# Down projection of a decoder block: PSUM banks copied by ScalarE and added by accumulating DMAs, and a seven-product scheme on 4 of 8 row blocks

## The chip, the cores and the metric

The kernel runs on one core of a Trainium2 chip. The metric is the device time of one execution in microseconds (us).

## The reference, cut to what matters

One layer of a hybrid decoder on 256 tokens of width 2048, in float32: three token mixers, merged by gates, and then a squared-ReLU MLP. The change touches the MLP's second half alone, the down projection from 8192 to 2048.

```python
h = rmsnorm(x, norm_ffn_g[l])
x = x + jnp.square(jax.nn.relu(h @ w_up[l])) @ w_down[l]     # w_up 2048x8192, w_down 8192x2048
return rmsnorm(x, final_g)
```

## The kernel before

Every matmul multiplies float32 numbers that are split into a high part (rounded to the float32r type) and a low part (the remainder); a product of two such numbers is three matmuls: high by high, high by low, low by high. TensorE (PE) does only these.

**Slabs.** All weights stream from HBM in slabs of 512 KB through a ring of four places in `w_raw`. For each slab, in order: SyncE issues the load (`load_slab`), ScalarE (ACT) copies the raw slab to `w_hi` (`hi`, L504), VectorE (DVE) writes `w_lo` as raw minus high (`lo`, L736), and PE multiplies (12 matmuls in the down projection). At PE's slab k, ACT and DVE prepare slab k+3 (`LOOKAHEAD`). The load of slab s is issued once `lo` of slab s-4 is done. Every engine walks the same loops (`walk`) in the order in which the code is written; each works through its own list, and semaphores join them.

**The MLP** runs in 4 chunks of 2048 hidden columns. A chunk has 4 trips of the up projection (`up`, 8 slabs each, two groups of 4: `n` = 0 and 1) and 2 trips of the down projection (`down`, 16 slabs each; a trip is called a pair here, since it makes two blocks of 512 output columns, `n` = 0 and 1, in turn, in the order of `PAIR` and `PAIR_ENDS`). When an up group ends, ACT copies half of its sums (`second`, L667), and DVE runs a chain over it: add (L1207), scale (L1209, which frees the PSUM banks: `evac_done`), squared ReLU (L1258), for n = 1 also the sums of activations that the seven-product scheme takes (`a_sums`, L808 to L813, and their low part, L818), and the low part of the hidden values (L1264).

**The seven-product scheme.** Two slabs of the same rows, of column blocks 0 and 1, hold four 128x512 blocks; with the two token blocks that is a 2x2 by 2x2 block product. It takes 8 products, 24 matmuls; `products_quad` takes 7, 21 matmuls, after a scheme of the Strassen-Winograd kind. It needs sums of weights: DVE makes four (`forms_first`, L747; `forms_second`, L754 and L757) into `w_sums`, ACT copies them to their high part (`forms_hi`, L510 and L512), and DVE takes the low part (`forms_lo`, L763, in two parts). A place where two slabs are done so is called a quad and named by its first slab in the trip; `quads` lists them. Of a quad's products three go into the corner banks (4 to 7) and four into banks of their own (P1, P6, P7, P5 in banks 0 to 3), which are added into several blocks of the output at the end of the trip.

**The sums at the end of a pair** are DVE's: `corner_sums` adds banks 4 to 7 to the token rows `y_tok` (L797, twice), `token_sums` adds P1, P5, P6 and P7 (L779 to L790, six instructions) after ACT has copied P1 (`first_product`, L519).

PE waits for `lo_done` at each slab, for `t_lo` (the forms' low part) at the second and the sixth product of a quad, and for `evac_done` at the first slab of each column block.

Of the kernel before, what the change touches and what calls it, by code (L numbers as in the profile page):

```python
# [27 lines left out]
P = 128  # L28
# [81 lines left out]
PAIR = [(0, 0), (0, 1), (1, 0), (1, 1), (0, 2), (1, 2), (0, 3), (1, 3), (0, 4), (1, 4), (0, 5), (1, 5)]  # L110
# [4 lines left out]
P_SUMS = 5  # L115
# [14 lines left out]
def quads(ph, c, t):  # L130

    if ph.name != "down":
        return ()
    return (6,) if last_trip(ph, c, t) else (6, 10, 14)


def quad_of(ph, c, t, k):

    return c * (3 * PH["down"].trips) + t * 3 + quads(ph, c, t).index(k)
# [23 lines left out]
def walk(eng, body):  # L163

    def loop(name, c=0, first=0):
        with eng.Fori(first, PH[name].trips) as t:
# [12 lines left out]
    for t in range(PH["A"].trips):  # L179
        body(PH["A"], 0, t)  # L180
    for t in range(PH["mix"].trips):
        body(PH["mix"], 0, t)
    def chunk(c):
        body(PH["up"], c, 0)
        loop("up", c, first=1)
        for t in range(PH["down"].trips):
            body(PH["down"], c, t)

    chunk(0)
    with eng.Fori(1, CHUNKS - 1) as c:  # L190
        chunk(c)
    chunk(CHUNKS - 1)
# [16 lines left out]
def build(nc, x, norm_mix_g, w_in, gate_b, conf_dw, conf_ln_g, conf_ln_b, w_conf_out, sconv_w,  # L209
# [5 lines left out]
    with ctx:  # L215
# [62 lines left out]
        v_now = sb("v_now", [P, 2, HD])  # L278
        mask = sb("mask", [P, SC])
# [51 lines left out]
        c_full, p_one, p_sum, p_last = sem("c_full"), sem("p_one"), sem("p_sum"), sem("p_last")  # L331
        gf_in, y_sq, y_gain = sem("gf_in"), sem("y_sq"), sem("y_gain")
# [153 lines left out]


        @block.scalar
        def _(act):
# [24 lines left out]
            def first_product(ph, c, t, k):  # L514

                if not (isinstance(c, int) and c == 0 and isinstance(t, int) and t == 0):
                    act.wait_ge(p_sum, P_SUMS * pair_of(c, t))
# [111 lines left out]
            def trip(ph, c, t):  # L629
                if ph == "v tokens":  # L630
                    return
                for k in range(ph.nslabs):
                    hi(ph, c, t, k)
                    forms_hi(ph, c, t, k)
                    if ph.name == "down" and k == quads(ph, c, t)[-1] + 1:
# [73 lines left out]
                    if last_trip(ph, c, t):  # L709
                        if k in (3, 4):  # L710
                            act.wait_ge(p_sum, P_SUMS * pair_of(c, t))
                            for b in range(2):
                                y_squared(b, k - 3, 2 * (k - 3) + b)
# [10 lines left out]
        def _(dve):  # L724
# [40 lines left out]

            def token_sums(c, t):

                base = P_SUMS * pair_of(c, t)
                g = group_of(PH["down"], c, t, 0)
                last = last_trip(PH["down"], c, t)  # L770
                cols = [bass.ds(t * 2 * DCOLS + n * DCOLS, DCOLS) for n in range(2)]
                rows2 = y_tok[:, 1, bass.ds(t * 2 * DCOLS, 2 * DCOLS)].rearrange("p (n w) -> p n w", n=2)
                p6, p7, p5 = (acc[:, P_BANK[name], :] for name in ("P6", "P7", "P5"))
                read, count = (p_last, 1) if last else (half_sum, 2)
                dve.wait_ge(p_one, pair_of(c, t) + 1)
                dve.wait_ge(slab_used, slab_of(PH["down"], c, t, quads(PH["down"], c, t)[-1] + 1) + 1)
# [14 lines left out]

            def corner_sums(c, t):

                for n in range(2):
                    cols = bass.ds(t * 2 * DCOLS + n * DCOLS, DCOLS)
                    dve.wait_ge(c_full, pair_of(c, t) * 2 + n + 1)
                    dve.tensor_tensor(y_tok[:, :, cols], acc[:, 4 + 2 * n:6 + 2 * n, :], y_tok[:, :, cols],  # L797
                                      ALU.add).then_inc(evac_done, 1)
# [214 lines left out]
            def final_block(c, t):  # L1013
# [33 lines left out]
                dve.wait_ge(p_sum, P_SUMS * (pair_of(c, t) + 1))  # L1047
# [16 lines left out]
                scale(1, 0)  # L1064

            def trip(ph, c, t):
# [4 lines left out]
                for k in range(ph.nslabs):  # L1071
# [22 lines left out]
                    if ph.name == "up" and k == 0 and isinstance(t, int) and not (isinstance(c, int) and c == 0):  # L1094
                        token_sums(c - 1, PH["down"].trips - 1)
                    if k + 4 in quads(ph, c, t):
                        forms_first(ph, c, t, k + 4)
# [8 lines left out]
                    if last_trip(ph, c, t):  # L1106
                        if k == 8:
                            token_sums(c, t)
                        if k in (9, 10):
                            dve.wait_ge(p_sum, P_SUMS * pair_of(c, t))  # L1110
# [168 lines left out]
        def _(pe):  # L1279
# [75 lines left out]
            def products_quad(ph, c, t, k):  # L1355
# [34 lines left out]
                if first and not (isinstance(c, int) and c == 0 and isinstance(t, int) and t == 0):  # L1390
                    pe.wait_ge(p_sum, pair_of(c, t) * P_SUMS)
# [217 lines left out]
```

## Time and profile before

| | us |
|---|---|
| median of 3 runs | 1515.77 (1515.49 to 1516.7) |
| the profiled execution | 1514.95 |
| its span | 1513.2 |
| PE busy | 1502.0 |
| DVE busy | 1188.9 |
| ACT busy | 755.7 |
| GpSimd (POOL) busy | 2.0 |

The span runs from the first to the last instruction of the profiled execution; its own time is 1.75 us longer. Busy times of PE are of overlapping, pipelined matmuls.

### The profile page before, as it was taken

To read this page: it belongs to the slowest core of one execution; us is meant where nothing else is said; L and a number is where in the kernel's file an instruction comes from. 1 tells how busy PE (TensorE), PEld (TensorE's weight loads), DVE (VectorE), ACT (ScalarE), POOL (GpSimd) and SP (SyncE) were. 2 spreads that over 40 slices of the span, in tenths; PEclk is the share of its full clock that TensorE was granted. 3 is DMA by queue.
4 is the path that set the end of the run, shared out by engine and by line. 5 is a ranking of instruction groups with operands and counts; after the bars stand their busy time and mean duration, and the time that the engine had idled before them with its cause. 6 is when DMAs were issued, how large, how long until landed. Compare 5 with 4: busy or idle time off the path is not lost.

```text
span 1513.2 us, 22156 instructions
## 1 busy us (share of the span) xinstructions
PE 1502.0 (99%) x7645; PEld 1267.4 (84%) x7645; DVE 1188.9 (79%) x1573; ACT 755.7 (50%) x940; POOL 2.0 (0%) x11
## 2 busy tenths in 40 slices
PE   9999999999999999999999999999999999999997
PEld 7888888877778888888888888888888888888886
DVE  6668889988889877565656779987799778987797
ACT  6444444465554455444445445544554545544554
POOL 0000000000000000000000000000000000000000
PEclk9999999999999999999999999999999999999999
DMA  7655666655555666665555565655556555556563
GB/s 251 190 187 185 192 194 195 199 177 173 171 173 192 192 197 208 195 200 191 189 185 167 184 205 203 201 182 193 190 199 207 182 192 196 208 181 208 195 219 144
DMA packets 209967, 290.94 MB, mean 192 GB/s; under 512 B 9227, under 2 KB 129107, under 8 KB 209778
## 3 DMA queue, kind: packets, MB, share of 16 engines
q1 hardware_dynamic: 209906, 290.14, 58.6%
q8 instruction: 37, 0.61, 0.2%
q14 instruction: 24, 0.20, 0.0%
HBM read 287.48 MB, written 2.10 MB: 191 GB/s over the span
## 4 chain that ended last, share of the span: by engine, by line
PE 99%; DVE 0%; ACT 0%; DMA 0%; issue 0%; DVEq 0%; ACTq 0%
PE acc L1309 27%; PE acc L1328 16%; PE acc L1330 15%; PE acc L1329 15%; PE acc L1307 13%; PE acc L1376 2%; PE acc L1377 2%; PE acc L1375 2%; PE acc L1302 2%; PE acc L1399 1%; PE acc L1304 1%; PE acc L1453 0%; PE acc L1475 0%; PE acc L1349 0%; PE acc L1348 0%; PE acc L1347 0%
## 5 line engine op out<-in xcount | busy, mean ns | idle before, releaser
L504 ACT ACTIVATE w_hi<-w_raw 128x1024 fp32r<-128x1024 f32 x511 | 534.0, 1057 | 477.4 <-PE acc L1330 285.3
L736 DVE TENSOR_TENSOR w_lo<-w_raw,w_hi 128x1024 fp32r<-128x1024 f32 x511 | 616.7, 1222 | 180.4 <-ACT w_hi L504 176.2
L1309 PE MATMUL acc<-h_hl,w_hi 128*128 128x512 f32 x1740 | 546.7, 395 | 0.0
L1307 PEld LDWEIGHTS acc<-h_hl,w_lo 128*128 128x128 f32 x1740 | 322.3, 188 | 72.4 <-issue 0.6
L1307 PE MATMUL acc<-h_hl,w_lo 128*128 128x256 f32 x1740 | 343.6, 279 | 0.0
L1309 PEld LDWEIGHTS acc<-h_hl,w_hi 128*128 128x128 f32 x1740 | 265.2, 189 | 0.0
L1328 PE MATMUL acc<-w_hi,m_hl 128*128 128x512 f32 x448 | 174.6, 390 | 0.0
L1330 PE MATMUL acc<-w_hi,m_hl 128*128 128x512 f32 x448 | 174.3, 389 | 0.0
L1329 PE MATMUL acc<-w_lo,m_hl 128*128 128x512 f32 x448 | 174.3, 389 | 0.0
L1328 PE MATMUL acc<-w_hi,h_hl 128*128 128x512 f32 x384 | 151.5, 394 | 0.0
L1330 PE MATMUL acc<-w_hi,h_hl 128*128 128x512 f32 x384 | 149.6, 389 | 0.0
L1329 PE MATMUL acc<-w_lo,h_hl 128*128 128x512 f32 x384 | 149.5, 389 | 0.0
L876 DVE SCALAR_TENSOR_TENSOR conv<-glu,par,conv (+1 forms) x240 | 109.1, 481 | 7.0 <-DVE conv L876 5.8
L1329 PEld LDWEIGHTS acc<-w_lo,m_hl 128*128 128x128 f32 x448 | 84.1, 188 | 17.4
L1330 PEld LDWEIGHTS acc<-w_hi,m_hl 128*128 128x128 f32 x448 | 84.1, 188 | 17.4
L1328 PEld LDWEIGHTS acc<-w_hi,m_hl 128*128 128x128 f32 x448 | 84.1, 188 | 17.4
L1328 PEld LDWEIGHTS acc<-w_hi,h_hl 128*128 128x128 f32 x384 | 72.1, 188 | 17.1 <-DVE w_lo L736 2.7
L667 ACT ACTIVATE second<-acc 128x512 f32<-128x512 f32 x58 | 34.7, 599 | 101.9 <-PE acc L1309 101.9
L1330 PEld LDWEIGHTS acc<-w_hi,h_hl 128*128 128x128 f32 x384 | 72.1, 188 | 15.2
L1329 PEld LDWEIGHTS acc<-w_lo,h_hl 128*128 128x128 f32 x384 | 72.1, 188 | 14.6
L1207 DVE TENSOR_TENSOR pair<-acc,second 128x512 f32<-128x512 f32 x54 | 37.3, 691 | 55.3 <-ACT second L667 55.3
L704 ACT ACTIVATE m_hl<-pair 128x512 f32 (+1 forms) x32 | 20.2, 632 | 73.6 <-DVE pair L1258 73.6
(208 smaller groups left out, 1472.9 us busy)
## 6 DMA issues: line engine op xcount, KB each, us to landing
w_raw<-in_w_in SPq DMA_DIRECT2D x200, 512.0 KB, 3.6
w_raw<-in_w_up SPq DMA_DIRECT2D x128, 512.0 KB, 4.3
w_raw<-in_w_down SPq DMA_DIRECT2D x128, 512.0 KB, 4.1
w_raw<-in_w_mix_out SPq DMA_DIRECT2D x32, 512.0 KB, 3.5
w_raw<-in_w_sconv_out SPq DMA_DIRECT2D x16, 512.0 KB, 4.2
w_raw<-in_w_attn_out SPq DMA_DIRECT2D x16, 512.0 KB, 3.6
w_raw<-in_w_conf_out SPq DMA_DIRECT2D x16, 512.0 KB, 4.6
bias_row<-in_gate_b SPq DMA_DIRECT2D x12, 256.0 KB, 4.0
```

The costliest lines, as they stand in the source:

```text
L504: act.activation(w_hi[:, q], w_raw[:, q], ACT.Copy).then_inc(hi_done, 1)
L667: act.activation(second[:, :, :], acc[:, b:b + 2, SEQ:], ACT.Copy).then_inc(half_copied, 1)
L736: dve.tensor_tensor(w_lo[:, q], w_raw[:, q], w_hi[:, q].bitcast(F32), ALU.subtract).then_inc(lo_done, 1)
L876: dve.scalar_tensor_tensor(dst, src, w, dst, ALU.mult, ALU.add).then_inc(step, 1)
L1207: dve.tensor_tensor(dst, halves[0], second[:, :, :], ALU.add).then_inc(half_sum, 1)
L1302: pe.matmul(*wide[m], start=True, stop=False)
L1307: pe.matmul(*narrow[m], start=False, stop=False)
L1309: last = pe.matmul(*wide[m], start=False, stop=final)
L1328: pe.matmul(acc[:, b + m, :], h_h, hi[:, a, :], start=first, stop=False)
L1329: pe.matmul(acc[:, b + m, :], h_h, lo[:, a, :], start=False, stop=False)
L1330: last = pe.matmul(acc[:, b + m, :], h_l, hi[:, a, :], start=False, stop=final)
L1375: pe.matmul(acc[:, at, :], rows[0], columns[0], start=start, stop=False)
```

## The change

The last two of an up chunk's slabs and the last two of a down trip now carry the forms of the next trip's first quad (`next_block`), so that each pair but the very last has quads at slabs 2, 6, 10 and 14 in place of 6, 10 and 14: that is 4 of 8 row blocks. `PAIR` changes the order of the first four slabs for that: column block 1 is begun at slab 1 in place of slab 2. The last up trip of a chunk is taken out of the loop. The very last pair keeps its one quad and its sums on DVE.

For the other seven pairs, `corner_sums` and `token_sums` are replaced. ACT copies banks 4 to 7 at slab 15 (`corner_copies`, two instructions) and P1 and P5 at slab 0 of what follows (`p_copies`, two). DVE makes P1+P6 and P1+P6+P7 (`partial_sums`, two). GpSimd issues eight accumulating DMAs a pair, from SBUF to SBUF: two of 512 KB, then three of 256 KB once these two have landed, then three of 256 KB once those have. ACT's next corner copies wait until all eight have landed, and so do the closing sums of the last pair.

The diff, cut to its core:

```diff
-PAIR = [(0, 0), (0, 1), (1, 0), (1, 1), (0, 2), (1, 2), (0, 3), (1, 3), (0, 4), (1, 4), (0, 5), (1, 5)]
+PAIR = [(0, 0), (1, 0), (0, 1), (1, 1), (0, 2), (1, 2), (0, 3), (1, 3), (0, 4), (1, 4), (0, 5), (1, 5)]
...
-    return (6,) if last_trip(ph, c, t) else (6, 10, 14)
+    return (6,) if last_trip(ph, c, t) else (2, 6, 10, 14)
...
         body(PH["up"], c, 0)
-        loop("up", c, first=1)
+        loop("up", c, first=1, last=1)
+        body(PH["up"], c, PH["up"].trips - 1)
...
+            def add_to(dst, src):
+                pool.dma_start(dst, src, accum_op=ALU.add).then_inc(y_acc, 16)
+
+            def trip(ph, c, t):
+                before = 16 * ADDS * pair_of(c, t)
+                cols = [slice((2 * t + n) * DCOLS, (2 * t + n + 1) * DCOLS) for n in range(2)]
+                for n in range(2):
+                    pool.wait_ge(evac_done, group_of(ph, c, t, n) + 1)
+                    add_to(y_tok[:, :, cols[n]], corner[n][:, :, :])
+                pool.wait_ge(p_copied, 2 * pair_of(c, t) + 2)
+                pool.wait_ge(y_acc, before + 32)
+                add_to(y_tok[:, 0, cols[0]], p1_copy[:, :])
+                for b in range(2):
+                    add_to(y_tok[:, b, cols[1]], p5_copy[:, :])
+                pool.wait_ge(p_sum, pair_of(c, t) + 1)
+                pool.wait_ge(y_acc, before + 80)
+                add_to(y_tok[:, 0, cols[1]], p16[:, :])
+                for n in range(2):
+                    add_to(y_tok[:, 1, cols[n]], p167[:, :])
...
+            def corner_copies(c, t):
+
+                if not (isinstance(c, int) and c == 0 and t == 0):
+                    act.wait_ge(y_acc, 16 * ADDS * pair_of(c, t))
+                for n in range(2):
+                    act.wait_ge(c_full, pair_of(c, t) * 2 + n + 1)
+                    act.activation(corner[n][:, :, :], acc[:, 4 + 2 * n:6 + 2 * n, :], ACT.Copy).then_inc(evac_done, 1)
+
+            def p_copies(c, t):
+
+                act.wait_ge(slab_used, slab_of(PH["down"], c, t, 15) + 1)
+                act.activation(p1_copy[:, :], acc[:, P_BANK["P1"], :], ACT.Copy).then_inc(p_copied, 1)
+                act.activation(p5_copy[:, :], acc[:, P_BANK["P5"], :], ACT.Copy).then_inc(p_copied, 1)
...
+            def partial_sums(c, t):
+
+                g = group_of(PH["down"], c, t, 0)
+                dve.wait_ge(p_copied, 2 * pair_of(c, t) + 2)
+                dve.tensor_tensor(p16[:, :], acc[:, P_BANK["P6"], :], p1_copy[:, :], ALU.add).then_inc(half_sum, 2)
+                dve.wait_ge(half_sum, g + 2)
+                dve.tensor_tensor(p167[:, :], acc[:, P_BANK["P7"], :], p16[:, :], ALU.add).then_inc(p_sum, 1)
...
+            def next_block(ph, t, k):
+
+                if ph.name == "up" and isinstance(t, int) and t == ph.trips - 1 and k >= ph.nslabs - 2:
+                    return PH["down"], 0, k - ph.nslabs
+                if ph.name == "down" and t < ph.trips - 1 and k >= ph.nslabs - 2:
+                    return ph, t + 1, k - ph.nslabs
+                return ph, t, k
...
-                    if k + 3 in quads(ph, c, t):
-                        forms_second(ph, c, t, k + 3)
-                    if ph.name == "down" and k == 15 and not last_trip(ph, c, t):
-                        corner_sums(c, t)
+                    down, to, at = next_block(ph, t, k)
+                    if at + 3 in quads(down, c, to):
+                        forms_second(down, c, to, at + 3)
                     lo(ph, c, t, k)
                     if ph.name == "down" and k == 0 and t:
-                        token_sums(c, t - 1)
+                        partial_sums(c, t - 1)
...
-                    if k + 4 in quads(ph, c, t):
-                        forms_first(ph, c, t, k + 4)
+                    if at + 4 in quads(down, c, to):
+                        forms_first(down, c, to, at + 4)
                     if k + 2 in quads(ph, c, t):
                         forms_lo(ph, c, t, k + 2, 0)
```

What this does to DVE's list is shown where a chunk passes from up to down (chunk 0). Before, the last up trip is in a loop (its end is the branch of L166), and the down trip begins with three `lo` and the forms of quad 6:

```order
600 L818 ISA [waits f_hi]
601 L818 TENSOR_TENSOR a_forms<-pair,a_forms 128x512
602 L166 REGISTER_ALU
603 L166 COMPARE_AND_BRANCH
604 L736 TENSOR_TENSOR w_lo<-w_raw,w_hi 128x1024 [waits hi_done] x3
605 L747 TENSOR_TENSOR w_sums<-w_raw 128x1024 [waits raw_full3,raw_full2]
606 L754 TENSOR_TENSOR w_sums<-w_raw,w_sums 128x512 [waits t_raw]
607 L757 TENSOR_TENSOR w_sums<-w_raw,w_sums 128x512 [waits t_two]
608 L736 TENSOR_TENSOR w_lo<-w_raw,w_hi 128x1024 [waits hi_done]
609 L733 TENSOR_TENSOR w_lo<-w_raw,w_hi 128x512 [waits hi_done]
610 L763 TENSOR_TENSOR w_forms<-w_sums,w_forms 128x1024 [waits t_hi]
```

In the changed kernel the end of the last up trip reads on DVE as follows (L786 is `lo`, L797 to L807 the forms' sums, L1257 the first step of the chain after an up group):

```order
609 L786 TENSOR_TENSOR w_lo<-w_raw,w_hi 128x1024 [waits hi_done] x3
610 L797 TENSOR_TENSOR w_sums<-w_raw 128x1024 [waits raw_full3,raw_full2]
611 L804 TENSOR_TENSOR w_sums<-w_raw,w_sums 128x512 [waits t_raw]
612 L807 TENSOR_TENSOR w_sums<-w_raw,w_sums 128x512 [waits t_two]
613 L786 TENSOR_TENSOR w_lo<-w_raw,w_hi 128x1024 [waits hi_done]
614 L1257 TENSOR_TENSOR pair<-acc,second 128x512 [waits half_copied,slab_used]
615 L1259 TENSOR_TENSOR pair<-pair,rstd 128x512 [waits half_sum]
616 L1308 SCALAR_TENSOR_TENSOR pair<-pair 128x512 [waits evac_done]
```

Three instructions on `w_sums` now stand between the sixth and the last `lo` of the up trip. Behind the chain follow, still on DVE, its last two steps, the first `lo` of the down trip (half a slab, L783) and the low part of the forms (L813):

```order
621 L1314 TENSOR_TENSOR m_hl<-pair,m_hl 128x2x256 [waits hid_hi]
622 L862 TENSOR_TENSOR a_forms<-pair,a_forms 128x512 [waits f_hi]
623 L783 TENSOR_TENSOR w_lo<-w_raw,w_hi 128x512 [waits hi_done]
624 L813 TENSOR_TENSOR w_forms<-w_sums,w_forms 128x1024 [waits t_hi]
625 L786 TENSOR_TENSOR w_lo<-w_raw,w_hi 128x1024 [waits hi_done]
626 L813 TENSOR_TENSOR w_forms<-w_sums,w_forms 128x1024 [waits t_hi]
627 L786 TENSOR_TENSOR w_lo<-w_raw,w_hi 128x1024 [waits hi_done]
```

On PE, the changed kernel's list from the third slab of that first down trip on (L1425 to L1427 are a quad's matmuls; `w_forms` in a row is a form of the weights):

```order
2510 L1380 MATMUL acc<-w_hi,m_hl 128x512
2511 L1425 MATMUL acc<-w_hi,m_hl 128x512 [waits lo_done,hid_lo]
2512 L1426 MATMUL acc<-w_lo,m_hl 128x512
2513 L1427 MATMUL acc<-w_hi,m_hl 128x512
2514 L1425 MATMUL acc<-w_forms,m_hl 128x512 [waits t_lo]
2515 L1426 MATMUL acc<-w_forms,m_hl 128x512
```

The wait for `t_lo` stands before the 28th matmul of the trip now; before, the first one stood before the 76th.

## Rows read from the trace of the kernel before

**Rows 1.** The page: the span, and PE's busy time, share and instructions.

```profile
span 1513.2 us, 22156 instructions
PE 1502.0 (99%) x7645; PEld 1267.4 (84%) x7645; DVE 1188.9 (79%) x1573; ACT 755.7 (50%) x940; POOL 2.0 (0%) x11
```

**Rows 2.** Waits of PE: the latest of its three (total, times, longest us).

```profile
PE acc L1302 <- DVE w_lo L829: 0.4, 1, 0.4
```

**Rows 3.** Timeline of PE: first matmuls of chunk 0's down and quad (start, us).

```profile
904.10 0.39 PE L1328 MATMUL acc<-w_hi,m_hl 128*128 128x512 f32 x1
...
920.43 0.39 PE L1375 MATMUL acc<-w_hi,m_hl 128*128 128x512 f32 x1
```

**Rows 4.** Line L1377: matmuls with a form of weights and plain activations.

```profile
L1377 PE MATMUL acc<-w_forms,m_hl x22: 389/389/389, 921.6 to 1479.9; 128*128 128x512 f32 x22
```

**Rows 5.** Timeline of DVE from the end of chunk 0's up on.

```profile
905.01 0.69 DVE L1207 TENSOR_TENSOR pair<-acc,second 128x512 f32<-128x512 f32 x1 [1.18 <-ACT second L667]
905.74 0.69 DVE L1209 TENSOR_TENSOR pair<-pair,rstd 128x512 f32<-128x512 f32 x1
...
909.96 3.50 DVE L736 TENSOR_TENSOR w_lo<-w_raw,w_hi 128x1024 fp32r<-128x1024 f32 x3
914.79 1.23 DVE L747 TENSOR_TENSOR w_sums<-w_raw 128x1024 f32<-128x1024 f32 x1 [1.34 <-DMA w_raw<-in_w_down]
...
917.39 1.22 DVE L736 TENSOR_TENSOR w_lo<-w_raw,w_hi 128x1024 fp32r<-128x1024 f32 x1
918.52 0.68 DVE L733 TENSOR_TENSOR w_lo<-w_raw,w_hi 128x512 fp32r<-128x512 f32 x1
919.13 1.22 DVE L763 TENSOR_TENSOR w_forms<-w_sums,w_forms 128x1024 fp32r<-128x1024 f32 x1
```

**Rows 6.** Timeline of ACT over the same stretch.

```profile
908.88 2.94 ACT L504 ACTIVATE w_hi<-w_raw 128x1024 fp32r<-128x1024 f32 x3
...
917.50 1.07 ACT L510 ACTIVATE w_forms<-w_sums 128x1024 fp32r<-128x1024 f32 x1 [1.62 <-DVE w_sums L757]
```

**Rows 7.** The load issued at 899.01, its landing, and that of the load at 901.28.

```profile
899.01 0.37 SPq L413 DMA_DIRECT2D w_raw<-in_w_down  x1
DMA to landing us min/median/max: 3.5/3.5/3.5
DMA to landing us min/median/max: 5.5/5.6/5.7
```

**Rows 8.** Timeline of DVE between chunk 0's two pairs.

```profile
942.19 1.22 DVE L736 TENSOR_TENSOR w_lo<-w_raw,w_hi 128x1024 fp32r<-128x1024 f32 x1 [0.36 <-ACT w_hi L504]
943.33 2.35 DVE L797 TENSOR_TENSOR y_tok<-acc,y_tok 128x1024 f32<-128x1024 f32 x2
...
948.09 0.68 DVE L779 TENSOR_TENSOR y_tok<-p_part,y_tok 128x512 f32<-128x512 f32 x1
...
953.14 2.36 DVE L736 TENSOR_TENSOR w_lo<-w_raw,w_hi 128x1024 fp32r<-128x1024 f32 x2
```

**Rows 9.** Timeline of ACT and of PE in the same place.

```profile
944.78 0.58 ACT L519 ACTIVATE p_part<-acc 128x512 f32<-128x512 f32 x1
945.85 1.06 ACT L504 ACTIVATE w_hi<-w_raw 128x1024 fp32r<-128x1024 f32 x1 [0.50 <-PE acc L1377]
945.59 0.39 PE L1328 MATMUL acc<-w_hi,m_hl 128*128 128x512 f32 x1
```

**Rows 10.** Busy times over the second pair (PE, PEld, DVE, ACT, POOL; clock, DMA share, GB/s).

```profile
945.80:986.90 41.10, 41.10 (x183) 34.02 (x182) 38.40 (x39) 22.08 (x23) 0.00 (x0) 1.00 0.61 199
```

**Rows 11.** DMA issues: the copies from SBUF to SBUF, KB each, us to landing.

```profile
k_dup<-pair SPq DMA_DIRECT2D x4, 128.0 KB, 2.4
```

**Rows 12.** Timeline of DVE: last sums of the last but one pair, first of the last.

```profile
1460.45 2.35 DVE L797 TENSOR_TENSOR y_tok<-acc,y_tok 128x1024 f32<-128x1024 f32 x2
...
1486.03 0.68 DVE L779 TENSOR_TENSOR y_tok<-p_part,y_tok 128x512 f32<-128x512 f32 x1
```

**Rows 13.** PE's last matmul, and the us in which its granted clock fell.

```profile
1505.08 0.39 PE L1349 MATMUL acc<-w_hi,m_hl 128*128 128x512 f32 x1
1508.00:1509.00 1.00, 0.00 (x0) 0.00 (x0) 0.75 (x1) 0.95 (x1) 0.00 (x0) 0.70 0.03 8
```

More of the change, by code:

```diff
@@ L114 @@
 S1, S2, S3, S4 = range(4)
-P_SUMS = 5
+ADDS = 8
 def last_trip(ph, c, t):
@@ L133, in quads @@
         return ()
-    return (6,) if last_trip(ph, c, t) else (6, 10, 14)
+    return (6,) if last_trip(ph, c, t) else (2, 6, 10, 14)
 def quad_of(ph, c, t, k):
-    return c * (3 * PH["down"].trips) + t * 3 + quads(ph, c, t).index(k)
+    return c * (4 * PH["down"].trips) + t * 4 + quads(ph, c, t).index(k)
 def pair_of(c, t):
@@ L163, in walk, with loop @@
 def walk(eng, body):
-    def loop(name, c=0, first=0):
-        with eng.Fori(first, PH[name].trips) as t:
+    def loop(name, c=0, first=0, last=0):
+        with eng.Fori(first, PH[name].trips - last) as t:
             body(PH[name], c, t)
@@ L278, in build @@
         v_now = sb("v_now", [P, 2, HD])
+        copies_at = nc.lookup_mloc(probs).addr
+        assert [nc.lookup_mloc(b).addr - copies_at for b in (probs_t, q_now, k_now)] == [4 * 1536, 4 * 2304, 4 * 2816]
+        corner = [view(f"corner{n}", probs, 2 * n * DCOLS, [P, 2, DCOLS]) for n in range(2)]
+        p1_copy, p5_copy = (view(f"p{i}_copy", probs, (4 + n) * DCOLS, [P, DCOLS]) for n, i in enumerate((1, 5)))
+        p16, p167 = (view(f"p_{i}", k_dup, n * DCOLS, [P, DCOLS]) for n, i in enumerate(("two", "three")))
         mask = sb("mask", [P, SC])
@@ L485, in _ @@
                                fill=MASKED, base=-1, pattern=[[1, BLK]], channel_multiplier=-1).then_inc(consts, 1)
+            def add_to(dst, src):
[16 more added lines that the diff above has]
+                    add_to(y_tok[:, 1, cols[n]], p167[:, :])
+            for c in range(CHUNKS):
+                for t in range(PH["down"].trips):
+                    if not last_trip(PH["down"], c, t):
+                        trip(PH["down"], c, t)
         @block.scalar
@@ L632, in trip @@
                 for k in range(ph.nslabs):
+                    if ph.name == "down" and k == 15 and not last_trip(ph, c, t):
+                        corner_copies(c, t)
                     hi(ph, c, t, k)
+                    if ph.name == "down" and k == 0 and t:
+                        p_copies(c, t - 1)
+                    if ph.name == "up" and k == 0 and isinstance(t, int) and t == 0 and not (isinstance(c, int) and c == 0):
+                        p_copies(c - 1, PH["down"].trips - 1)
                     forms_hi(ph, c, t, k)
-                    if ph.name == "down" and k == quads(ph, c, t)[-1] + 1:
+                    if last_trip(ph, c, t) and k == quads(ph, c, t)[-1] + 1:
                         first_product(ph, c, t, k)
@@ L1390, in products_quad @@
                 if first and not (isinstance(c, int) and c == 0 and isinstance(t, int) and t == 0):
-                    pe.wait_ge(p_sum, pair_of(c, t) * P_SUMS)
+                    pe.wait_ge(p_sum, pair_of(c, t))
+                    pe.wait_ge(p_copied, 2 * pair_of(c, t))
                 product(P_BANK["P1"], whole(0, 2 * i), loaded(w_x, 0), first, final).then_inc(slab_used, 1)
```

42 lines of the change are left out of this document (14 added, 28 removed).

## The prediction

> **What bounds the kernel now.** The page comes first: PE is busy for 1502.0 of 1513.2 us [rows 1]. Its waits come next, since a busy share alone doesn't say that nothing is lost: the latest wait of PE is at the first slab of all [rows 2], so from about 11 us to its last matmul at 1505 us PE never stops. Time is then the number of matmuls times their spacing. The spacing is read from the timeline, not from the 0.39 us of one, as they overlap: from 904.10 to 920.43 there are six slabs of 12, so 16.33 / 72 = 0.227 us [rows 3]. All other engines matter only where they would make PE wait, and for that the question is always the same: when is a thing ready, and when does PE ask for it?
>
> **What it takes away.** A quad saves 3 matmuls of 24. The line of the quads' third matmuls counts 22 quads, by the one form-by-plain product in each [rows 4]: 7 pairs of 3 and one of 1. With 4 in each of 7 pairs it is 29. So 7 x 3 x 0.227 = 4.76 us less, 0.31% of the time. That is all that can be won; the sums that leave DVE (2.3 us at 943.33 and 5.05 us from 948.09 to 953.14 in each pair [rows 8]) are work beside PE and worth nothing by themselves. A measurement of this kernel can tell about 0.2%, 3 us, from no change.
>
> **The new first quad, up to down.** This is the place on which I stake the number. Call 904.10 the start of the down trip in chunk 0 [rows 3]. PE asks for the forms at its 28th matmul, 904.10 + 27 x 0.227 = 910.22. When are they ready? DVE goes through its list in order:
> - the forms' first sum needs the slab that was issued at 899.01 and landed 3.5 us later [rows 7], so it starts at about 902.6;
> - from such a sum to the `lo` behind the second sums it is 917.39 - 914.79 = 2.60 us, and that `lo` takes 1.13 to the next instruction [rows 5]: the chain after the up group, which began at 905.01, begins at 906.33, that is 1.32 us late;
> - the chain lasts 909.96 - 905.01 = 4.95 us [rows 5]: 911.28;
> - half a `lo` 0.61 (918.52 to 919.13), the forms' low part 1.22 [rows 5]: 913.11.
>
> ACT is no earlier: its first copy behind the chain began at 908.88, with the shift 910.20; half a copy of about 0.6 and the forms' copy of 1.07 [rows 6] give 911.87, just when DVE wants it. So PE stands for 913.11 - 910.22 = 2.89 us. Part of it is paid earlier: column block 1 is now begun at slab 1, at 904.10 + 12 x 0.227 = 906.82, and its banks are freed when L1209 ends, at 906.43 before and 907.75 with the shift [rows 5], so 0.93 us at slab 1 and the other 1.96 at the quad. It isn't added, since DVE's chain doesn't wait for these slabs. After it, the second part of the forms (one `lo` of 1.13 and 1.22 more: 915.4) is asked for 12 matmuls after 913.11, at 915.8, so it holds by 0.4 us. The other chunks have the same list: 4 x 2.89 = 11.6 us.
>
> Bounds of this term: with the slab there in time the chain isn't shifted at all, and 905.01 + 4.95 + 0.61 + 1.22 = 911.79 still leaves 1.57 us, 6.3 in all. With the landing of 5.6 us that a load behind two others took [rows 7] it is 2.1 us more, 5.0 each and 20 in all. I take 3.5 us, as this very load had it alone in flight.
>
> **The new first quad, down to down** (4 times). DVE's `lo` at 942.19 ends its step at 943.33 [rows 8]. Then: the sums of the forms 2.60, a `lo` 1.13, half a one 0.61, `partial_sums` two adds of 0.72, the low part 1.22: 950.3. PE asks at 945.59 + 27 x 0.227 = 951.7 [rows 9], so 1.4 us are left. ACT has two corner copies of 1.06 where it had nothing, and two bank copies of 0.58 where it had one [rows 9]; from c_full at about 942.4 its list is copy, copy, high part (to 945.6), half a high part at 945.85 [rows 9], two bank copies, forms (to 948.7), each before DVE needs it. The next quad needs DVE for about 9.1 of PE's 10.2 us. Cost: nothing; if the cover is gone, each us of DVE's lateness beyond 1.4 is a us of PE, four times. PE's wait for the P banks (`p_copied`, `p_sum`, done by 949.1) is 9 matmuls into the quad, at 953.1, and costs nothing.
>
> **The accumulating DMAs.** The trace has none. A pair adds 2 x 512 + 6 x 256 KB, 2.62 MB. Over a pair the loads keep the DMA engines 61% busy at 199 GB/s [rows 10], so 326 GB/s when busy, and 2.62 MB are 8.0 us of all 16 engines if an add costs as a load does. The spare time in a pair is 0.39 x 41.1 = 16.0 us. So they fit, even where an add costs twice; from there on they don't. A copy from SBUF to SBUF took 2.4 us to land [rows 11]; three rounds of that with 8 us of transfer are some 15 to 20 us. ACT asks for them a pair later (41 us), and in the last pair DVE asks at 1486.03, 25.6 us after the corner sums of the pair before [rows 12]. I take nothing for it; the other end, twice the cost and loads pushed back, is a rival below.
>
> The Trainium skill ("Collectives: The Full Stack", The bandwidth ceiling) says that an add in the DMA engines needs two source reads where a copy needs one and so runs at half the rate. By it a pair's adds would be 16 us of all engines, and the spare time would be just used up; no row here shows an add. The Trainium skill ("SBUF — State Buffer", SBUF: two separate sides) also says that VectorE's two-port modes lock GpSimd out while it writes descriptors; the instructions of DVE in the down trips are adds of two tensors, 1.22 us for 1024 columns, which show no such mode, so by it nothing would be late.
>
> **The sum.** 1514.95 - 4.76 + 11.6 = 1521.8 for an execution like the profiled one, which lay 0.8 us below the median; against the median 1522.6. The last up trip is out of its loop, which spares a few tenths of register work in its chain. Predicted: 1522 us, 0.4% slower.
>
> **Rivals.**
> - *Slower still, by the DMA engines* (12 in 100). Where an add costs twice, pairs with adds beside quads are full, the loads' landing goes from 3.5 towards 5.6 us and more, and DVE, which already waited for a slab at 914.79, gets late: against it, the spare 1.4 us and the reading above; for it, bursts of loads landed at 5.6 us even before. If four pairs lose a tenth of their 41 us, 16 us: 1538. A few us in the last pair alone (DVE waits for the adds) would be 1526.
> - *Slower still, by the clock* (8 in 100). PE has no stop in the trace after the start; at the end its granted clock fell in the us after 1508, some 2.9 us after its last matmul had ended [rows 13]. A stop of 2.9 us in two parts, with work between them, is hardly that. If it fell, the 18 matmuls left of the quad would go at 1.2 in place of 2.4 GHz, 4.1 us a chunk: 1538.
> - *No change* (12 in 100). The stop is near its lower bound of 1.57 us, since the slab is early: 4 x 1.57 - 4.76 is +1.5 us, 1517.
> - *Faster* (13 in 100). The forms are ready in time: 1511. It would need DVE's way from 905.01 to the low part to be 5.2 us where the rows add to 6.8 without any shift; it is decided at 1.19 us of stop in each chunk, the point at which stops and saving are equal. For it speaks only that DVE and ACT lose other work there, and the token sums before were far from this place.
> - *My forecast* (55 in 100): 1517.5 to 1526, most at 1522.
>
> Slower by over 0.2% (above 1518.8) hold the forecast and the first two rivals: 0.75. Within 0.2%: 0.12. Faster: 0.13. The range leaves out the fast case and the worst of the slow ones: 1514 to 1530.
>
> **What would show it.** Waits of PE in the changed trace: for DVE's `w_forms` (L813) four times at about 2 us, and at the second slab of each chunk's first down trip for about 0.9 us; DVE's chain L1257 beginning 1.3 us later after the slab before the down trip; first sums (L797) idle for a DMA there. No wait of PE between the two pairs of a chunk. 29 quads at L1427. Loads landing at about 4 us. The prediction is wrong if PE shows no waits there, or if the longest waits are for slabs (`lo`) in the pairs.

## The result, and the profile after

The changed kernel took 1530.93 us (median of 4 runs, 1530.8 to 1534.11) against 1515.99 us (4 runs, 1515.49 to 1516.7) on the same chip: a ratio of 1.0104, 95% interval 1.0092 to 1.0116. It is slower by 15 us where 7 were predicted, and 0.9 us beyond the range. The profiled execution took 1530.8 us.

The page of the changed kernel, its span, PE's busy time, two DMA queues (packets, MB, share of 16 engines) and the landing of the largest adds (KB each, median us from issue to landing):

```profile
span 1529.0 us, 22058 instructions
PE 1503.1 (98%) x7624; PEld 1263.3 (83%) x7624; DVE 1177.2 (77%) x1566; ACT 781.0 (51%) x975; POOL 55.6 (4%) x67
...
q1 hardware_dynamic: 209906, 290.14, 59.7%
q0 software_dynamic: 9856, 18.35, 6.9%
...
y_tok<-corner POOLq DMA_DIRECT2D x14, 512.0 KB, 8.8
```

PE has its 21 matmuls less than in [rows 1] (7645 to 7624) and is not less busy. The last matmul, at 1505.08 before [rows 13], now starts at 1521.18 (the last row of PE's timeline below). It is 16.10 us later although 21 x 0.227 = 4.77 us of work are gone: PE stands 20.9 us more than before. I call this sum the *stops* of a kernel (the shift of its last matmul against 1505.08, plus 0.227 us for each matmul fewer than 7645; up to 0.6 us of it is the start, which differs from run to run). It is the quantity that every experiment below takes apart. The waits of PE name the first places (us in all, times, longest):

```profile
PE acc L1378 <- DVE pair L1259: 5.4, 4, 2.0
PE acc L1425 <- DVE w_forms L813: 5.2, 5, 1.5
PE acc L1397 <- DVE w_lo L786: 3.5, 3, 2.1
```

Where [rows 2] ended at the first slab, there are now waits for VectorE in three kinds of place. They don't add to 20.9, since this view leaves small waits out, so I also went along PE's timeline and took every start that came over 0.227 us behind the one before: 13.4 us at the first quads of the four chunks (the large ones are 2.15 and some 1.75 in chunk 0, the latter spread over matmuls at the lower clock, and 1.41 + 1.62, 1.29 + 1.64, 1.23 + 1.57 in the others), 2.1 us in the second pairs of chunks 0 to 2, where the large ones stand at the quad of slab 6 and none at that of slab 2, and 4.4 us at the closing products of the last pair.

**The timelines.** That of DVE at chunk 0's way from up to down, at its second pair, and ahead of the last token sums (start, us, the idle time before in brackets):

```profile
897.97 3.50 DVE L786 TENSOR_TENSOR w_lo<-w_raw,w_hi 128x1024 fp32r<-128x1024 f32 x3 [0.26 <-ACT w_hi L536]
904.04 1.23 DVE L797 TENSOR_TENSOR w_sums<-w_raw 128x1024 f32<-128x1024 f32 x1 [2.57 <-DMA w_raw<-in_w_down]
...
907.77 0.68 DVE L1257 TENSOR_TENSOR pair<-acc,second 128x512 f32<-128x512 f32 x1
...
913.13 1.23 DVE L813 TENSOR_TENSOR w_forms<-w_sums,w_forms 128x1024 fp32r<-128x1024 f32 x1 [0.17 <-ACT w_forms L542]
...
960.69 1.23 DVE L797 TENSOR_TENSOR w_sums<-w_raw 128x1024 f32<-128x1024 f32 x1 [3.41 <-DMA w_raw<-in_w_down]
...
1496.58 1.22 DVE L786 TENSOR_TENSOR w_lo<-w_raw,w_hi 128x1024 fp32r<-128x1024 f32 x1 [0.62 <-ACT w_hi L536]
1502.09 0.69 DVE L833 TENSOR_TENSOR y_tok<-p_part,y_tok 128x512 f32<-128x512 f32 x1 [4.29 <-DMA y_tok<-p_three]
```

and of PE, in chunk 0 and at the end:

```profile
906.95 0.39 PE L1380 MATMUL acc<-w_hi,m_hl 128*128 128x512 f32 x1
909.33 0.47 PE L1378 MATMUL acc<-w_hi,m_hl 128*128 128x512 f32 x1 [1.99 <-DVE pair L1259]
...
911.31 0.63 PE L1379 MATMUL acc<-w_lo,m_hl 128*128 128x512 f32 x1
...
914.43 0.48 PE L1425 MATMUL acc<-w_forms,m_hl 128*128 128x512 f32 x1
...
1508.42 0.50 PE L1397 MATMUL acc<-w_hi,m_hl 128*128 128x512 f32 x1 [2.15 <-DVE w_lo L786]
...
1521.18 0.39 PE L1399 MATMUL acc<-w_hi,m_hl 128*128 128x512 f32 x1
```

From up to down the mechanism is the predicted one: the slab for the first sum is waited for, the chain after the up group starts late (907.77 instead of 905.01 [rows 5]), and PE stands at the second slab for its banks.

In the second pair DVE waits 3.41 us for a load at the first sum of the quad at slab 6. In the last pair it waits for an add, and PE then for the slab's low part behind it. Where that add was, the chain that ended last shows (start, us, what):

```profile
1470.89 1.95 ACT corner L557 x2
1472.84 0.71 POOL y_tok L495
1473.55 10.68 DMA y_tok<-corner
1484.27 0.51 issue
1484.78 1.12 POOL y_tok L495 x2
1485.90 5.77 DMA y_tok<-p_copy
1491.71 0.49 issue
1492.20 1.08 POOL y_tok L495 x2
1493.28 8.79 DMA y_tok<-p_three
1502.09 0.69 DVE y_tok L833
```

The three rounds of adds take 28.5 us, from 1473.55, when the second add of the first round starts, to 1502.07. DVE asked for them at 1496.58 + 1.22 = 1497.80. Two of DVE's waits in all (us, times, longest):

```profile
DVE w_sums L797 <- DMA w_raw<-in_w_down: 30.7, 19, 3.4
DVE y_tok L833 <- DMA y_tok<-p_three: 4.3, 1, 4.3
```

The first of them is the other trace of the adds. The first sums of the quads waited 10.5 us in 15 places before (L747); now it is 30.7 us in 19. The load behind the wait of 3.41 us was issued at 951.43, while two adds of 512 KB were under way (issued at 947.40 and 948.31, landed at 953.38 and 958.27). From issue to landing it took, in the changed kernel and in e1 below, which has no adds and issues it at 951.55:

```profile
DMA to landing us min/median/max: 9.1/9.1/9.1
DMA to landing us min/median/max: 4.9/4.9/4.9
```

### The profile page after: what moved, and what is told of

The parts are those of the page before. It is cut to its first block, busy times and chain, and to the rows that moved or that the text cites. A ratio compares the mean times of both kernels' runs of the same rounds, so it can differ in the third digit from the quotient of the medians.

```text
span 1529.0 us, 22058 instructions
## 1 busy us (share of the span) xinstructions
PE 1503.1 (98%) x7624; PEld 1263.3 (83%) x7624; DVE 1177.2 (77%) x1566; ACT 781.0 (51%) x975; POOL 55.6 (4%) x67
## 3 DMA queue, kind: packets, MB, share of 16 engines
q0 software_dynamic: 9856, 18.35, 6.9%
## 4 chain that ended last, share of the span: by engine, by line
PE 82%; DMA 8%; DVE 7%; issue 2%; ACT 1%; SPq 0%; POOL 0%; DVEq 0%; ACTq 0%; POOLq 0%
PE acc L1359 25%; PE acc L1357 12%; PE acc L1378 12%; PE acc L1380 12%; PE acc L1379 12%; DMA w_raw<-in_w_down 6%; DVE w_lo L786 2%; PE acc L1352 2%; PE acc L1425 2%; PE acc L1426 1%; PE acc L1427 1%; DVE w_sums L797 1%; PE acc L1450 1%; PE acc L1354 1%; DVE w_sums L804 1%
## 5 line engine op out<-in xcount | busy, mean ns | idle before, releaser
L536 ACT ACTIVATE w_hi<-w_raw 128x1024 fp32r<-128x1024 f32 x504 | 527.1, 1056 | 462.0 <-PE acc L1380 258.2
L786 DVE TENSOR_TENSOR w_lo<-w_raw,w_hi 128x1024 fp32r<-128x1024 f32 x504 | 609.9, 1222 | 197.8 <-ACT w_hi L536 189.6
L1378 PE MATMUL acc<-w_hi,m_hl 128*128 128x512 f32 x392 | 153.8, 392 | 5.4 <-DVE pair L1259 5.4
L1380 PE MATMUL acc<-w_hi,m_hl 128*128 128x512 f32 x392 | 153.2, 391 | 0.0
L1379 PE MATMUL acc<-w_lo,m_hl 128*128 128x512 f32 x392 | 153.0, 390 | 0.0
L1378 PEld LDWEIGHTS acc<-w_hi,m_hl 128*128 128x128 f32 x392 | 73.7, 188 | 22.1 <-issue 3.8
L1380 PEld LDWEIGHTS acc<-w_hi,m_hl 128*128 128x128 f32 x392 | 73.9, 189 | 15.5
L1379 PEld LDWEIGHTS acc<-w_lo,m_hl 128*128 128x128 f32 x392 | 73.9, 188 | 15.2
L1378 PEld LDWEIGHTS acc<-w_hi,h_hl 128*128 128x128 f32 x384 | 72.1, 188 | 17.1 <-DVE w_lo L786 2.7
L1380 PEld LDWEIGHTS acc<-w_hi,h_hl 128*128 128x128 f32 x384 | 72.1, 188 | 15.2
L813 DVE TENSOR_TENSOR w_forms<-w_sums,w_forms 128x1024 fp32r<-128x1024 f32 x58 | 70.7, 1219 | 0.7 <-ACT w_forms L542 0.7
L1257 DVE TENSOR_TENSOR pair<-acc,second 128x512 f32<-128x512 f32 x54 | 37.3, 690 | 42.5 <-ACT second L717 42.4
```

Source lines behind the costliest of these rows:

```text
L536: act.activation(w_hi[:, q], w_raw[:, q], ACT.Copy).then_inc(hi_done, 1)
L786: dve.tensor_tensor(w_lo[:, q], w_raw[:, q], w_hi[:, q].bitcast(F32), ALU.subtract).then_inc(lo_done, 1)
L813: dve.tensor_tensor(w_forms[:, 1, two, :], w_sums[:, two, :], w_forms[:, 0, two, :].bitcast(F32), ALU.subtract).then_inc(t_lo, 1)
L1257: dve.tensor_tensor(dst, halves[0], second[:, :, :], ALU.add).then_inc(half_sum, 1)
L1378: pe.matmul(acc[:, b + m, :], h_h, hi[:, a, :], start=first, stop=False)
L1379: pe.matmul(acc[:, b + m, :], h_h, lo[:, a, :], start=False, stop=False)
```

## The experiments

All times are medians, each ratio is against the kernel before on the same chip (1515.0 to 1516.0 us). By the intervals of the ratios, the difference between two kernels is uncertain by some 3 us; the stops come from one profiled execution of each and say where the time is. They are worked out as above. The very last pair has one quad in every kernel, so 4 + 4 is 29 quads, 3 + 4 is 25 and 3 + 3 the 22 of before.

| kernel | quads in the two pairs of a chunk | token sums by | us | ratio, 95% | stops |
|---|---|---|---|---|---|
| changed | 4 + 4 | adding DMAs | 1530.9 | 1.0104 [1.0092, 1.0116] | 20.9 |
| e1 | 4 + 4 | left out | 1523.7 | 1.0053 [1.0036, 1.0070] | 13.8 |
| e2 | 4 + 4 | copying DMAs | 1523.4 | 1.0056 [1.0039, 1.0073] | 13.2 |
| e3 | 3 + 4 | adding DMAs | 1522.1 | 1.0039 [1.0025, 1.0053] | 10.3 |
| e4 | 3 + 3 | adding DMAs | 1522.2 | 1.0033 [1.0019, 1.0048] | 7.5 |
| e5 | 4 + 4 | DMAs, last two pairs DVE | 1526.0 | 1.0069 [1.0052, 1.0085] | 15.8 |
| e6 | 4 + 4, reordered | as e5 | 1521.2 | 1.0039 [1.0024, 1.0053] | 11.9 |
| e7 | 3 + 4 | as e5 | 1516.1 | 1.0009 [0.9999, 1.0018] | 2.1 |
| e8 | 4 + 4 | DVE, all | 1543.1 | 1.0185 [1.0168, 1.0202] | 32.6 |
| e9 | as e6 | GpSimd's own adds | 1543.1 | 1.0185 [1.0171, 1.0199] | 33.0 |
| e10 | as e7 | GpSimd's own adds | 1536.4 | 1.0137 [1.0122, 1.0153] | 24.6 |
| e11 | 4 + 4 | GpSimd's own adds | 1546.9 | 1.0208 [1.0193, 1.0224] | 38.1 |
| e12 | as e6 | left out | 1515.3 | 1.0002 [0.9993, 1.0011] | 5.4 |

My theory was that two things lose the time: the first quad of a chunk, which comes before its forms are ready, and the adds, through the weight loads and through the last pair. The rivals: the adds cost nothing and all is VectorE's lateness; or the last pair alone is the adds' price.

**e1: no adds.** The pairs' additions and the waits on them are left out.

```
-                    if not last_trip(PH["down"], c, t):
+                    if False:
                         trip(PH["down"], c, t)
```

> The changed kernel without the eight accumulating DMAs of each pair and without the waits for them (what they add is missing from the output); the quads, the copies by ScalarE and the partial sums stay. Theory: the adds cost 4.4 us in the last pair, where VectorE waits for them, and about 2 us in the four second pairs through late loads, while the stop of about 3 us at each chunk's first quad comes from VectorE's order alone and stays: 1524 to 1525 us. Rival: the adds' traffic delays everything, the forms at the first quad too: 1518 or less.

1523.74 us. All the stops that are left are at the first quads (2.13 + 1.56, 1.34 + 1.64, 1.04 + 1.61, 1.16 + 1.58); those in the second and the last pairs are gone. DVE's waits for loads at the first sums:

```profile
DVE w_sums L794 <- DMA w_raw<-in_w_down: 12.0, 10, 2.6
```

So the adds cost 1530.9 - 1523.7 = 7.2 us, a little more than expected, and the first quads about 13. Both halves of the theory stand.

**e2: the same DMAs, copying instead of adding.**

```
-                pool.dma_start(dst, src, accum_op=ALU.add).then_inc(y_acc, 16)
+                pool.dma_start(dst, src).then_inc(y_acc, 16)
```

> The changed kernel with plain copies in place of the adding DMAs, same queue, sizes and waits (the token rows are overwritten where they should be added to, so the output is another). Theory: adding is what is dear, it keeps the DMA engines busy about twice as long per byte as a load; as copies the software queue falls from 6.9% of the engines to about 3.8%, a 512 KB transfer lands in 4 to 6 us in place of 8.8, the three rounds end before the last pair asks for them, and 4 to 6 us go: 1525 to 1527 us. Rival: GpSimd's writing of descriptors (about 1.2 us an issue) and the waits between rounds make them late: the landing stays near 8 us and the time at 1530 to 1531 us.

1523.43 us, no more than with no DMAs at all: 1.6 us under the low end of what I expected. Same bytes, same issues on GpSimd, same rounds; only the adding is gone. The page of e2:

```profile
q0 software_dynamic: 5376, 18.35, 3.1%
```

An added MB takes 6.9/3.1 = 2.2 times the engines' time of a copied one, in 1.8 times the packets. The corner banks land in 5.7 instead of 8.8 us, and DVE's waits at the first sums are 18.1 us, between e1's 12.0 and the changed kernel's 30.7. The rounds of the last but one pair, 28.5 us with adds, take 23.0 (1469.94 to 1492.89) and are over before VectorE asks. What costs is the adding itself: the issue on GpSimd and the order in three rounds are the same here and stop nothing.

**e3: no quad at slab 2 of a chunk's first down pair.**

```
-    return (6,) if last_trip(ph, c, t) else (2, 6, 10, 14)
+    if last_trip(ph, c, t):
+        return (6,)
+    return (2, 6, 10, 14) if t else (6, 10, 14)
```

> The changed kernel with quads at 6, 10 and 14 in the first pair of each chunk and at 2, 6, 10 and 14 in the second (the last pair keeps its one). Theory: the four stops at the chunks' first quads go (4 x 3.1 us, and up to 1.7 us of slow clock in one of them), four quads of 0.68 us come back: 1519 to 1521 us. Rival (the adds are what costs): the stops were only where lateness showed; it shows again at the next quad, and the time stays above 1527 us.

1522.08 us, the stops between up and down gone. These four quads save 4 x 0.68 = 2.7 us and cost 11.6 (1530.9 - 1522.1 = 8.8 net). It is 1 us above what I expected; the last pair's stop of closing products grew from 2.31 to 3.58 us, as it comes earlier while the adds' rounds take as long.

**e4: the old three quads with the new sums.** Here nothing is saved and nothing new is asked of the first quads.

```
-    return (6,) if last_trip(ph, c, t) else (2, 6, 10, 14)
+    return (6,) if last_trip(ph, c, t) else (6, 10, 14)
```

> One part of the change alone: the sums by ScalarE's copies and the accumulating DMAs, with the quads of the kernel before (6, 10, 14). Theory: no stop at the chunks' first down trips, 4.4 us in the last pair, 0 to 1 us by late loads: 1520 to 1521.5 us, slower than before by that alone. Rival (adds cost some us in every pair): 1527 us or more. Second rival (the last pair's wait is hidden when the quads are as before): 1516 us.

1522.24 us, 0.7 us above the expected range. The new way to sum costs 6.3 us by itself by the medians, and 5.0 by the ratio, whose interval goes from 2.9 to 7.3 us (the five times lie between 1518.57 and 1523.26), even where VectorE has more time than before. The stops of the profiled execution are 0.61 us in the second pair of chunk 1, and 0.35 + 0.88 and 3.7 in the last pair.

**e5: the sums of the last two pairs by VectorE**, as before, and the adds elsewhere.

```
+            def by_dve(c, t):
+                return isinstance(c, int) and c == CHUNKS - 1 and isinstance(t, int) and t == 0
...
-                    if not last_trip(PH["down"], c, t):
+                    if not last_trip(PH["down"], c, t) and not by_dve(c, t):
```

> The changed kernel with the sums of the last but one pair alone made by VectorE, as in the kernel before, so that the last pair waits for no adding DMA of that pair. Theory: the closing part loses its 4.4 us: 1526 to 1527 us. Rival: the last pair's stops come from VectorE's own late work (the token sums at slab 8), not from the wait for the adds, and VectorE has more work now: 1531 us or more.

1526.01 us: 4.9 us less, by the stops of the last pair, which were 4.4.

**e6: e5 with the first quads' work moved.** The last steps of the up group's chain (`m_hl`, `a_forms`) go behind slabs 7 to 11 of the down trip, the forms' low parts ahead of other work, and the product that needs T4 is done later in a quad.

```
+                    if ph.name == "down" and t == 0:
+                        if k == A_AT:
+                            tail_a(c, PH["up"].trips - 1, 1)
+                        if k == B_AT:
+                            tail_b(c, PH["up"].trips - 1, 1)
```

> e5 with the order at each chunk's first quad changed and nothing left out: VectorE does only the first two steps of the chain after the last up group (add and scale, which frees the banks), then the forms' second sums and the slab's low part, then the forms' low parts; the rest of the chain waits for slabs 7 and 11 of the down trip, ScalarE's copies for it for slab 9; in a quad, TensorE takes the product with T4 fourth in place of second. Theory: the stops at the chunks' first quads (13 us) are only VectorE's order, so most go; VectorE is nearly full in the first pairs, so 0 to 1 us a chunk stays: 1513 to 1517 us, at or below the kernel before. Rival: VectorE has too much work for four quads in a pair that begins with the up chain; the stops only move to the next quads: 1522 us or more.

1521.17 us. The expectation failed, and the time is close to the rival's. The stops at the first quads are gone. But new ones stand in the second pairs: 1.18 + .41 us at 960.9, 2.36 + .47 at 1134.5, .76 + .45 at 1309.6, and .97 + .55 + .41 in the last chunk. DVE, which now had its moved work to do, waited for a load there; the row is from the timeline of e6:

```profile
958.37 1.22 DVE L821 TENSOR_TENSOR w_sums<-w_raw 128x1024 f32<-128x1024 f32 x1 [3.44 <-DMA w_raw<-in_w_down]
```

**e7: e3 and e5 together.**

> Both repairs that leave the order alone: no quad at 2 in the chunks' first pairs (e3) and the last but one pair summed by VectorE (e5). Theory: what the two took away is separate, so the gains add: 1522.1 - 5.0 = 1517 us (1516 to 1518), about 1 us slower than before for 3 quads more. Rival: e3 took VectorE's lateness away in the last pair too, and the gains overlap: 1519 us or more.

1516.1 us (10 runs, 1514.72 to 1518.03): 14.8 us below the changed kernel, and no different from before. The two gains add: 8.8 + 4.9 = 13.7. Three quads more than before save 2.0 us, and 2.1 us of stops take them back in the profiled execution, which was the fastest of the ten.

**e8: four quads, and all sums by VectorE as before.** The other half of the change alone; the lines are from its difference to the kernel before.

```
-    return (6,) if last_trip(ph, c, t) else (6, 10, 14)
+    return (6,) if last_trip(ph, c, t) else (2, 6, 10, 14)
```

> The other part of the change alone: quads at 2, 6, 10 and 14, with all sums by VectorE as before (no ScalarE copies of the corners, no adding DMAs). Theory: the four stops at the chunks' first quads stay (13 us), and between the pairs of a chunk VectorE has 7.3 us of sums before the forms of quad 2, so 4 to 7 us of stop three times more: 1536 to 1546 us. Rival (the sums fit beside PE there too): 1524 us, as without adds.

1543.1 us, inside the expected range. The fourth quad needs the time that the sums took of VectorE. The waits of PE in e8:

```profile
PE acc L1385 <- DVE w_forms L764: 12.2, 6, 2.6
PE acc L1338 <- DVE pair L1219: 5.5, 4, 2.7
PE acc L1338 <- DVE y_tok L798: 4.3, 3, 1.5
```

So taking the sums from VectorE was worth 12 us to four quads (1543.1 - 1530.9); what was wrong is where they went.

**e9, e10, e11: GpSimd adds by itself**, without a DMA, in e6, e7 and the changed kernel.

```
-                pool.dma_start(dst, src, accum_op=ALU.add).then_inc(y_acc, 16)
+                pool.tensor_tensor(dst, src, dst, ALU.add).then_inc(y_acc, 16)
```

> The kernel of e6 (first quads fed in time, last pair's sums by VectorE, 1521.2 us), in which GpSimd adds the copied banks to the token rows with its own tensor_tensor instead of issuing an accumulating DMA; nothing is left out. Theory (the adds' traffic delays the weight loads, and these stop TensorE in the second pairs of a chunk): those stops, some 7 us in e6, go, and the time is 1511 to 1515 us. Rival (GpSimd's additions hold VectorE up or come too late for the banks' copies): VectorE's times per form grow and new stops stand in the pairs; 1520 us or more.

> The kernel of e7 (no quad in the first down pair of a chunk, last pair's sums by VectorE, 1516.1 us), with GpSimd's own additions in place of the accumulating DMAs; nothing is left out. Theory: its three stops between pairs (0.4 to 0.75 us each) go, 1514 to 1515.5 us. Rival (GpSimd's additions disturb VectorE): 1518 us or more.

> The changed kernel with GpSimd's own additions in place of the accumulating DMAs and nothing else changed; nothing is left out. Theory (all that the adds cost is their traffic on the DMA engines and the time of the last rounds): about what the kernel without any adds had, 1523 to 1525 us, plus what GpSimd's own additions take behind the last bank, up to 3 us. Rival (additions of GpSimd slow VectorE): stops in the second pairs stay or grow, 1530 us or more.

1543.06, 1536.44 and 1546.91 us: the rival of all three. The loads come sooner (q0 is gone, DVE's waits at the first sums fall from 28.6, 24.0 and 30.7 us to 17.1, 12.5 and 13.8), but DVE is slowed. The timeline of e9 at the start of the second pair, DVE and then POOL:

```profile
943.61 1.22 DVE L810 TENSOR_TENSOR w_lo<-w_raw,w_hi 128x1024 fp32r<-128x1024 f32 x1
944.74 3.43 DVE L821 TENSOR_TENSOR w_sums<-w_raw 128x1024 f32<-128x1024 f32 x1
948.21 2.77 DVE L828 TENSOR_TENSOR w_sums<-w_raw,w_sums 128x512 f32<-128x512 f32 x1
951.01 1.65 DVE L831 TENSOR_TENSOR w_sums<-w_raw,w_sums 128x512 f32<-128x512 f32 x1
952.58 2.29 DVE L810 TENSOR_TENSOR w_lo<-w_raw,w_hi 128x1024 fp32r<-128x1024 f32 x1
```

```profile
943.65 6.77 POOL L508 TENSOR_TENSOR y_tok<-corner,y_tok 128x1024 f32<-128x1024 f32 x2 [940.89 <-ACT corner L572]
950.59 5.41 POOL L508 TENSOR_TENSOR y_tok<-p_copy,y_tok 128x512 f32<-128x512 f32 x3 [0.17 <-POOL y_tok L508]
```

The first DVE instruction above was already running when POOL's first one began, 0.04 us later, and takes its usual 1.22 us; the same sum that takes 1.23 us in e6 takes 3.43 beside them, a 512-column one 2.77 instead of 0.69. In e9 as a whole DVE is busy for 1230.7 us instead of e6's 1180.6, 50 us more beside 110.5 us of POOL. The Trainium skill ("SBUF — State Buffer", Who interferes with whom) says that an instruction of VectorE with two inputs in SBUF contends with one of GpSimd that reads SBUF; the trace agrees, as all of the slowed ones have two such inputs. An instruction of DVE with one of its inputs in PSUM (`acc`) keeps its usual time in the midst of POOL's:

```profile
1001.74 0.68 DVE L844 TENSOR_TENSOR p_two<-acc,p_copy 128x512 f32<-128x512 f32 x1
1000.90 5.56 POOL L508 TENSOR_TENSOR y_tok<-p_copy,y_tok 128x512 f32<-128x512 f32 x3 [0.17 <-POOL y_tok L508]
```

Part of what e8 to e11 lose is the clock's: during or behind their longer stops (2.7 to 3.9 us) PE's granted clock fell to 0.5, for 10.2 us in all in e8, 13.7 in e9, 23.9 in e10 and 20.5 in e11. The longest stretch of e10 (stretch, its length, busy us of PE, PEld, DVE, ACT and POOL with the instructions, granted clock, DMA share, GB/s):

```profile
1133.80:1144.10 10.30, 7.79 (x18) 5.64 (x19) 10.27 (x7) 2.73 (x3) 7.67 (x4) 0.50 0.44 154
```

In these stretches matmuls start 0.43 instead of 0.23 us apart, which sums to some 4 us in e8 and e9 and 7 us in e10 and e11. How much of that is lost isn't known, since part of it stands in front of a wait; no run separates it from VectorE's lateness.

**e12: e6 without adds.** It asks whether e6's stops came from the adds.

> The kernel of e6 without its accumulating DMAs and the waits on them, so that the output lacks the copied banks and the sums of the banks of the first seven pairs. It asks whether the stops that e6 had between its down pairs (some 7 us of 1521.2) come from the adds. Theory (the adds' traffic delays the weight loads, for which VectorE, now without slack, waits): those stops go, VectorE's waits for the loads in front of the block sums fall from 28.6 to about 12 us, and the time is 1511.5 to 1515 us. Rival (VectorE without slack is late by itself, whatever the DMA engines carry): the stops stay, 1518 to 1521 us.

1515.32 us (11 runs), 5.9 us less than e6, 0.3 above the expected range. The stops fall from 11.9 to 5.4 us, and DVE's waits at the first sums from 28.6 to 15.2:

```profile
DVE w_sums L819 <- DMA w_raw<-in_w_down: 15.2, 17, 3.4
```

Over half of e6's stops were the adds'. But the rest is not nothing: about 20 small stops of 0.1 to 0.6 us at the quads, 2.2 us of them in the last chunk, and together they take back just what the seven quads save (4.8 us). Even without any adding DMA, eight quads a chunk in this order are no faster than six.

## Why the prediction was wrong

**The saving.** 21 matmuls fewer, 0.227 us apart: as predicted.

**Up to down.** Predicted 2.89 us a chunk, 11.6 in all. Measured without the adds (e1): 3.7, 3.0, 2.7 and 2.7, 12.1 us by the large stops alone, where the changed kernel has 12.7, or 13.4 with the small ones; and e3 gives 11.6 by taking the quads out. This term holds. Its parts came out differently: the stop at slab 1 was 2.15 us in chunk 0 and 1.2 to 1.4 in the others instead of 0.93, that at the forms 1.6 to 1.75 instead of 1.96. In chunk 0 the cause is the load that I took at 3.5 us, as if alone in flight, though before, too, the next one was issued at 900.14, ahead of its landing. Now it was issued at 899.22 and there for DVE at 904.04, inside the bounds given (3.5 to 5.6). The tenths that the loop's end was said to spare did come: the chain took 912.27 - 907.77 = 4.50 us where it had taken 4.95.

**Down to down.** "Cost: nothing; 1.4 us slack". True without adds: e1 has no stop in a second pair. It held for the quad at slab 2 with them, too. But at the quad of slab 6 they made 2.1 us, the large ones (0.72, 0.45 and 0.24) behind loads for which DVE waited 3.41, 3.21 and 2.98 us.

**The accumulating DMAs. This is the step that failed**: "I take nothing for it". The experiments give 7.2 us (changed kernel against e1), 6.3 us (e4 against before; 5.0 by the ratio) and 5.9 us (e6 against e12). Of the 7.2, 4.4 us are the wait of the last pair, and 2.1 the late loads of the second pairs. With 13.4 in place of 11.6 us at the first quads, that is 8.3 of the 9 us by which the sum of 1521.8 fell short of the profiled 1530.8. Two of its numbers were mis-sized. I costed an add like a load, 8.0 us of 16 engines a pair; measured it is 6.9% of 1529.0 us over 7 pairs, 15.1 us. And I took 15 to 20 us for the three rounds, from a landing of 2.4 us in [rows 11], a transfer alone with free engines; it was 28.5 us, among the loads. The time at which DVE asks was right (25.6 us after; measured 1497.8 - 1472.8 = 25.0), so the last pair waited 4.3 us instead of having five to ten to spare. By the Trainium skill's rule for adds ("Collectives: The Full Stack", The bandwidth ceiling), half the rate of a copy, the estimate for a pair was 16 us; the trace agrees, with 15.1. The prediction wrote both sums down and chose the cheap one.

**The mean hid the late loads.** 15.1 us would still fit in the 16.0 us that [rows 10] leave free. But the adds are not spread over the pair: they begin with its end, when the loads for the next pair's first slabs are due. Such a load landed after 9.1 us in place of 4.9 and was waited for 3.41 us at 960.69. By the prediction VectorE was 1.4 us ahead of PE at the quad before and gained about 1.1 on it since, and indeed only 0.72 us of the 3.41 reached PE. "They fit" was said of a mean, and the price is paid at a point.

**Rivals.** The DMA engines' rival had the cause and, in its small form (a few us in the last pair alone), half the size; its 1538 was too much, as second pairs lost 0.1 to 0.9 us each and not 4. The clock's rival did happen, once, in chunk 0, and cost almost nothing (below). Neither the lower bound nor the faster case was near. Of the signs of being wrong that the prediction named, one came true: PE's longest wait, 2.1 us, is for a slab's low part (`lo`), in the last pair.

**What stays open.** What the last, small stops of e12 hang on was not tried one by one. A smaller or later spread of the adds wasn't tried either, so whether they would fit between the loads is not known.

## What to carry to other kernels

Cost an adding DMA at twice a copying one (2.2 times here), and look not at whether it fits in the mean but at which load is in flight beside it and who waits for that load. Work that is taken from a busy engine must go somewhere that the first one doesn't depend on: here the DMA engines feed VectorE and GpSimd reads SBUF beside it, and both gave the time back. Before products are saved at a phase's first slabs, count whether their forms can be ready: four quads there cost 11.6 us and saved 2.7.

## What the runs showed of the hardware

The granted clock fell behind a stop of 2.15 us in the middle of the program. Below are windows of the changed kernel (stretch, its length, busy us of PE, PEld, DVE, ACT and POOL with the instructions, granted clock, DMA share, GB/s):

```profile
907.00:910.70 3.70, 1.71 (x8) 1.19 (x7) 3.56 (x8) 0.63 (x1) 0.00 (x0) 1.00 0.39 137
910.70:914.10 3.40, 3.40 (x10) 2.65 (x9) 3.13 (x5) 3.10 (x5) 0.00 (x0) 0.50 0.04 8
914.10:918.00 3.90, 3.90 (x18) 3.02 (x18) 3.90 (x5) 2.90 (x3) 0.00 (x0) 1.00 0.71 219
```

PE stood from 906.95 + 0.39 to 909.33, worked for 1.4 us, and then went at 1.2 in place of 2.4 GHz for 3.4 us (starts 0.43 instead of 0.23 us apart). In e1, with a stop of 2.13 us at the same place, the clock stayed high:

```profile
910.70:914.10 3.40, 2.42 (x11) 1.67 (x9) 3.09 (x6) 2.99 (x5) 0.00 (x0) 1.00 0.03 13
```

There PE stood a second time, 1.56 us, in the same stretch. And in e3 PE stood 3.58 us in the last pair, and the clock stayed high through the stop and behind it (a row of PE's timeline, then windows):

```profile
1500.54 0.50 PE L1399 MATMUL acc<-w_hi,m_hl 128*128 128x512 f32 x1 [3.42 <-DVE w_lo L788]
1496.00:1500.00 4.00, 1.12 (x5) 0.58 (x4) 3.90 (x6) 3.87 (x7) 0.00 (x0) 1.00 0.01 4
1500.00:1504.00 4.00, 2.78 (x11) 1.98 (x12) 4.00 (x7) 0.00 (x0) 0.00 (x0) 1.00 0.00 0
```

So the length of a stop alone doesn't tell whether the clock falls. The changed kernel and e1 began with the forms at nearly the same moment, 914.43 and 914.52, when VectorE had them ready: here a slow clock in front of a wait cost nothing. And an added SBUF to SBUF transfer of 18.35 MB was 9856 packets and 6.9% of the engines, a copied one 5376 packets and 3.1%.
